# Projecting two kinds of keys with the weights stationary, so that they come out transposed

## What is computed

```
p = t @ w_in                       # t: the 256 tokens, and the same for the 256 context rows
qa, ka, va, qb, kb, vb, ob, g = split(p)          # six of width 512, ob, 16 gate columns
y_a = neighbourhood_attention(qa, ka, va, kax, vax, rpb)           # 8 heads of 64
h_b = mlstm_bidirectional(axial_rope(qb), axial_rope(kb) * k_scale, vb, li, lf,
                          qbx, kbx * k_scale, vbx, lix, lfx)       # 4 heads of 128
y = concat([y_a, mlstm_readout(h_b, ob, head_g)]) @ w_out
# axial_rope: of each pair (x[2d], x[2d+1]) of a head, with the angle of token and d
#   out[2d] = x1 * cos - x2 * sin;  out[2d+1] = x1 * sin + x2 * cos
```

## Time and profile before

| | |
|---|---|
| time, median of 3 executions | 1587.98 us (1587.47 to 1588.07) |
| time of the profiled execution | 1587.57 us |
| its span in the profile | 1585.7 us |
| granted TensorE clock, mean | 0.999 |
| busy: PE / DVE / ACT | 99% / 74% / 49% |
| instructions: PE / DVE / ACT | 7994 / 1917 / 1246 |

### The profile page before, as it was taken

One profiled execution on the slowest core, in us unless ns is written; L12 is line 12 of the kernel. 1 busy time (PEld: TensorE's weight loads), 2 busy tenths in 40 slices (PEclk: granted clock), 3 DMA queues, 4 the chain that ended last, 5 costly groups with the idle time before them and its releaser, 6 DMA issues.

```text
span 1585.7 us, 20742 instructions
## 1 busy us (share of the span) xinstructions
PE 1564.3 (99%) x7994; PEld 1296.7 (82%) x7994; DVE 1172.3 (74%) x1917; ACT 777.9 (49%) x1246; POOL 70.5 (4%) x112
## 2 busy tenths in 40 slices
PE   7999999999999999999999999999999999999998
PEld 5787778888888888887777888888888888888887
DVE  7889899759986665477766888868877667666654
ACT  5767666532222222254556555445555463455552
POOL 2000000100000000030010100000000100010000
PEclk9999999999999999999999999999999999999999
DMA  9987676336656655252122777857777685555550
GB/s 378 371 294 275 230 253 222 107 127 231 214 211 239 225 213 176 90 175 80 67 95 74 292 293 289 314 216 266 257 285 269 211 304 188 171 202 188 187 188 33
DMA packets 93044, 336.97 MB, mean 212 GB/s; under 512 B 10625, under 2 KB 11265, under 8 KB 92690
## 3 DMA queue, kind: packets, MB, share of 16 engines
q1 hardware_dynamic: 90706, 327.58, 57.5%
q0 software_dynamic: 2240, 8.06, 1.5%
HBM read 334.56 MB, written 1.05 MB: 212 GB/s over the span
## 4 chain that ended last, share of the span: by engine, by line
PE 55%; DVE 1%; ACT 1%; issue 0%; POOL 0%; POOLq 0%; DVEq 0%; ACTq 0%
PE bank L292 53%; PE bank L295 2%; DVE sb_tm L301 0%; ACT sb_XN L298 0%; DVE sb_X L301 0%; ACT sb_arena L298 0%; ACT sb_XC L298 0%; DVE sb_arena L319 0%; DVE sb_XN L301 0%; DVE sb_sg L316 0%; DVE sb_XC L301 0%; DVE sb_w7r L301 0%; DVE sb_w5r L301 0%; POOL sb_rstd L301 0%; DVE sb_rows L309 0%
## 5 line engine op out<-in xcount | busy, mean ns | idle before, releaser
L292 PE MATMUL bank<-sb_hT,sb_hi 128*128 128x512 f32 (+1 forms) x1856 | 574.9, 379 | 0.0
L298 ACT ACTIVATE sb_hi<-sb_w 128x1024 fp32r<-128x1024 f32 x428 | 431.3, 1052 | 281.8 <-DMA sb_w<-in_w 238.8
L292 PEld LDWEIGHTS bank<-sb_hT,sb_hi 128*128 128x128 f32 x1856 | 332.1, 188 | 58.5 <-issue 0.2
L292 PE MATMUL bank<-sb_hi,sb_hT 128*128 128x512 f32 x1152 | 369.6, 395 | 2.5 <-ACT sb_hT L298 1.3
L292 PEld LDWEIGHTS bank<-sb_hi,sb_hT 128*128 128x128 f32 x1152 | 215.6, 188 | 52.8 <-issue 5.3
L312 DVE CUSTOM_DVE_ANT_0 sb_w<-sb_w,sb_cb 128x1024 f32<-128x1024 f32 x144 | 174.7, 1218 | 0.0
L301 DVE TENSOR_TENSOR sb_sg<-bank,sb_sg 128x512 f32<-128x512 f32 (+1 forms) x90 | 58.9, 660 | 103.1 <-ACT sb_sg L298 82.2
L298 ACT ACTIVATE sb_sg<-bank 128x512 f32<-128x512 f32 (+1 forms) x98 | 55.0, 573 | 118.2 <-PE bank L292 117.7
L298 ACT ACTIVATE sb_arena<-bank 128x512 f32<-128x512 f32 (+1 forms) x106 | 56.4, 559 | 55.4 <-PE bank L292 32.3
L301 DVE TENSOR_TENSOR sb_tm<-bank,sb_rows 128x512 f32<-128x512 f32 (+1 forms) x41 | 28.1, 684 | 69.4 <-PE bank L292 66.5
L298 ACT ACTIVATE sb_XN<-sb_X 128x512 f32<-128x512 f32 x33 | 20.7, 629 | 99.2 <-DVE sb_X L301 91.3
(11 more groups left out here) (483 smaller groups left out, 3209.7 us busy)
## 6 DMA issues: line engine op xcount, KB each, us to landing
sb_w<-in_w SPq DMA_DIRECT2D x428, 512.0 KB, 4.3
sb_w<-in_mw SPq DMA_DIRECT2D x192, 512.0 KB, 4.7
sb_rows<-in_na_rpb POOLq DMA_DIRECT2D x16, 96.0 KB, 3.0
sb_X<-in_x SPq DMA_DIRECT2D x1, 1024.0 KB, 4.9
sb_cb<-in_cvec POOLq DMA_DIRECT2D x2, 512.0 KB, 8.8
sb_XC<-in_ctx POOLq DMA_DIRECT2D x1, 1024.0 KB, 13.0
sb_arena<-in_sg_ln_g POOLq DMA_DIRECT2D x1, 1024.0 KB, 7.1
sb_arena<-in_sg_ln_b POOLq DMA_DIRECT2D x1, 1024.0 KB, 10.4
```

The costliest lines, as they stand in the source:

```text
L292: return self.e.matmul(out, a, b, start=start, stop=stop)
L298: return self.e.activation(out, a, f, **kw)
```

## The change

Two kinds, mk and nk, are projected by a new function `pe_across`: the weights are stationary, the activations of the tokens and the context (both at once, 2 x 256 columns) are moving. Each of the four banks then holds 128 features on partitions and all 512 rows. The number of matmuls and their shape stay. No transposes, and no copies to `XN` and `XC`, are left for these kinds.

The memory keys' rotation then runs over partitions. The host permutes the columns of mq and mk in w_in, so that of each head the first members of the pairs lie in partitions 0 to 63 and the second ones in 64 to 127. `dve_keys` reads each pair of banks with three multiplications, one of 128 partitions by the cosine and two of 64 partitions that write the other half's partitions by the sine, and one sum. The table `axt` (128 x 512) comes by a new DMA on GpSimd's queue. ACT copies the context half of mk (`act_keys`). For nk, ACT copies each bank to `nkh` and DVE subtracts to `nkl`, after the last score of the mLSTM (`SCO ml 3 1`). Banks of mk are set free by the third multiplication of a pair, those of nk by the subtractions. The queries nq are split as soon as they are turned, behind tile 7. `sig`, the gate of the readout, moves to another place of the arena, so its evacuation waits for `PVS ml 3 1`.

```diff
-        MX = {5: [("cx", (0, 1))], 6: [("cx", (2, 3))], 7: [("t", ("nq", 0))], 8: [("gates", 0)],
-              9: [("gs", 0)], 10: [("t", ("mq", 0)), ("gs", 1)], 11: [("gs", 2)], 12: [("t", ("mk", 2)), ("t", ("mk", 0))],
-              13: [("pf", 0)]}
+
+
+        MX = {5: [("cx", (0, 1))], 6: [("cx", (2, 3))], 7: [("t", "nq")], 8: [("gates", 0)],
+              9: [("gs", 0)], 10: [("t", "mq"), ("gs", 1)], 11: [("gs", 2)], 13: [("pf", 0)]}
...
-        MX[20] += [("nqs", 0)]
-        MX[21] += [("t", ("nk", 0)), ("t", ("nk", 2)), ("nb", 0)]
+        MX[21] += [("nb", 0)]
...
+            if kind == "mk":
+                return (DE, "mk", "read", j // 2)
+            if kind == "nk":
+                return (DE, "nk", j)
+            return (AE, "mx", kind, j)
...
+                elif u < 28 and kind in ("mk", "nk"):
+                    pe_across(e, W_MX + u, key, at, BANK[key], ready)
                 elif u >= 4:
                     pe_unit(e, W_MX + u, key, parts, at, BANK[key], range(n), ready, first, last)
...
+        def pe_across(e, t, key, k0, banks, ready):
+
+
+            w, l = HI_[HB[t]], ring_r[SLOT["w", t]]
+            e.wait_ge(*done(HI, t))
+            for g in range(4):
+                c, b = slice(g * 128, g * 128 + 128), banks[g]
+                if k0 == 0:
+                    for f in b.free():
+                        e.wait_ge(*f)
+                for k in range(2):
+                    kc = k0 + k
+                    for f in ready(kc, "h", range(4)):
+                        e.wait_ge(*f)
+                    e.mm(b.ap[:, :], w[:, k, c], hTh[:, :, kc, :], kc == 0, False)
+                    for f in ready(kc, "l", range(4)):
+                        e.wait_ge(*f)
+                    e.mm(b.ap[:, :], w[:, k, c], hTl[:, :, kc, :], False, False)
+                    e.wait_ge(*done(LO, t))
+                    m = e.mm(b.ap[:, :], l[:, k, c], hTh[:, :, kc, :], False, kc == 7)
+                if g == 3:
+                    m.then_inc(USED.sem, USED.put(t))
+                    if k0 == 6:
+                        ENDED[(*key, g)] = (USED, t)
+                elif k0 == 6:
+                    m.then_inc(ACC.sem, ACC.put(*key, g))
+                    ENDED[(*key, g)] = (ACC, *key, g)
...
+        def act_keys(e, kind):
+            for g in range(4 if kind == "nk" else 2):
+                if kind == "nk":
+                    e.wait_ge(*ended("mx", "nk", g))
+                    e.act(nkh[:, g, :], BANK["mx", "nk"][g].ap[:, :], ACT.Copy).then_inc(AE.sem, AE.put("nk", g))
+                else:
+                    for j in (2 * g, 2 * g + 1):
+                        e.wait_ge(*ended("mx", "mk", j))
+                    e.act(mkT[:, 2 * g:2 * g + 2, 256:512], banks2[g][:, :, 256:512], ACT.Copy).then_inc(AE.sem, AE.put("mk", g))
+
+        def dve_keys(e, kind):
+            if kind == "nk":
+                e.wait_ge(*done(SCO, "ml", 3, 1))
+                for g in range(4):
+                    e.wait_ge(*done(AE, "nk", g))
+                    e.tt(nkl[:, g, :], BANK["mx", "nk"][g].ap[:, :], nkh[:, g, :].bitcast(F32), ALU.subtract).then_inc(
+                        DE.sem, DE.put("nk", g))
+                return
+            e.wait_ge(*done(LD["axt"], 0))
+            for g in range(2):
+                b, o = banks2[g][:, :, 0:256], mkT[:, 2 * g:2 * g + 2, 0:256]
+                w = TM[g].rearrange("p (a b) -> p a b", a=2)
+                co, si = (axt[:, i, :].unsqueeze(1).to_broadcast([128, 2, 256]) for i in range(2))
+                e.wait_ge(*done(AE, "mk", g))
+                e.wait_ge(DE, DE.n)
+                e.tt(o, b, co, ALU.mult).then_inc(DE.sem, DE.put("mk", "cos", g))
+                e.tt(w[0:64], b[64:128], si[64:128], ALU.mult).then_inc(DE.sem, DE.put("mk", "first", g))
+                e.tt(w[64:128], b[0:64], si[0:64], ALU.mult).then_inc(DE.sem, DE.put("mk", "read", g))
+                e.wait_ge(DE, DE.n)
+                e.tt(o, o, w, ALU.add).then_inc(DE.sem, DE.put("mk", g))
```

More of the change, by code:

```diff
@@ L2199, in build, with queries_ready, keys_ready, memory_ready @@
         MX[31] += [("gate", 0), ("y", 1)]
[L2201 to L2208, removed]
+        def queries_ready():
+            return [done(DE, "nq", 1)]
+        def keys_ready():
+            return [done(DE, "nk", 3)]
+        def memory_ready():
+            return [done(AE, "t", "mq", 0), done(DE, "t", "mq", 1), done(AE, "mk", 1), done(DE, "mk", 1)]
         def mx_tile(u):
@@ L2250, in pe_mixer @@
                     elif what == "t":
[L2251 to L2256, removed]
+                        w = [done(DE, "axial", "mq", 3)] if i == "mq" else [done(AE, "mx", "nq", j) for j in range(2)]
+                        pe_transposes(e, ("t", i), TQ[i == "mq"], 0, 4, w, TB,
+                                      lambda c2, i=i: ((DE, "nq", c2) if i == "nq" else (DE if c2 else AE, "t", "mq", c2),))
                     elif what == "pf":
@@ L2356, in pe_mlstm @@
                 if ph == 0:
-                    for f in all_turned("mq") + all_turned("mk"):
+                    for f in memory_ready():
                         e.wait_ge(*f)
@@ L2526, in pe_neighbour_scores @@
                 b = BANK["nS", i] = HB3.take()
-                for f in b.free() + [done(AE, "nqs"), done(DE, "nqs")] + all_turned("nk"):
+                for f in b.free() + queries_ready() + keys_ready():
                     e.wait_ge(*f)
@@ L2688, in act_mixer @@
                         act_gate_sums(e, i)
[L2689 to L2698, removed]
                     elif what == "t":
[L2700 to L2703, removed]
+                        for c2 in range(2 if i == "nq" else 1):
+                            e.wait_ge(*done(TRP, "t", i, c2))
+                            e.act((nqh if i == "nq" else mqT)[:, c2 * 2:c2 * 2 + 2, :], pair(BANK["t", i, c2]), ACT.Copy).then_inc(
+                                AE.sem, AE.put("t", i, c2))
                         act_tick(e, W_MX + u)
@@ L2803, in dve_mixer @@
                         dve_neighbour_bias(e, 1)
[L2804 to L2808, removed]
-                        for c2 in range(2):
[L2810 to L2815, removed]
+                    elif what == "t" and i == "nq":
+                        for c2 in range(2):
+                            c = slice(c2 * 2, c2 * 2 + 2)
+                            e.wait_ge(*done(AE, "t", "nq", c2))
+                            e.tt(nql[:, c, :], pair(BANK["t", "nq", c2]), nqh[:, c, :].bitcast(F32), ALU.subtract).then_inc(
+                                DE.sem, DE.put("nq", c2))
                     elif what == "t":
[L2817 to L2820, removed]
+                        e.wait_ge(*done(TRP, "t", "mq", 1))
+                        e.cp(mqT[:, 2:4, :], pair(BANK["t", "mq", 1])).then_inc(DE.sem, DE.put("t", "mq", 1))
                     elif what == "o":
@@ L3137 @@
     put("gb", a["ml_gate_b_2"].reshape(8, 2))
-    consts, blk, mlm = shape_constants()
+    consts, blk, mlm, axt = shape_constants()
+    mix = np.array(a["mix_w_in_2"])
+    for kind in ("mq", "mk"):
+        c = slice(BASE2[kind], BASE2[kind] + 512)
+        mix[..., c] = mix[..., c].reshape(-1, D, 4, 64, 2).transpose(0, 1, 2, 4, 3).reshape(-1, D, 512)
+    a = dict(a, mix_w_in_2=mix)
     w = np.stack([np.concatenate([a[name][ix][r:r + 256, n:n + 512 // len(ns)] for n in ns], axis=1)
```

63 lines of the change are left out of this document (31 added, 32 removed).

## The result

The changed kernel takes 1585.43 us (median of 21 runs, 1585.04 to 1585.97), the kernel before 1587.71 us (21 runs, 1587.45 to 1588.07): 2.28 us less, a ratio of 0.9985 with a 95% interval of 0.9979 to 0.9992. The forecast was 1585.5, 2.4 us less than before.

A forecast was written before the change was run, and what follows sets the result against it. PE, busy 99% of the span, was taken to bound the kernel. The terms -3.49 - 0.90 + 1.80 + 0.19 = -2.4 us gave 1585.5 us from a median of 1587.98; the 8-in-10 range was 1583.9 to 1587.2.

The forecast's parts named there:

- Transposes: PE, behind tiles 12 and 21: 32 transposes go, 16 at each, 1.75 and 1.74 us, in sum -3.49 us.
- Swapped operands: Tiles 8 to 11 and 16 to 19: 192 matmuls with weights stationary keep the 0.227 us pace, so 0.
- The rival of a slower pace: Swapped matmuls might not stream at 0.227 us; at 0.26 the kernel takes 1592 us; chance 0.05.
- Score block: Head 0's first score block: its waits for mkT's last copies and sb_fcol go, -0.90 us, bounds 0.5 and 0.9.
- Tile 12: New PE wait for banks freed by DVE's third multiplication, and again at the third bank: +1.80 us, between 1.36 and 2.16.
- The middle case: Tile 12: each DVE operation starts only when the one ahead has ended, 0.70 us apart, so three end at 722.27.
- Tile 20: PE waits for bank 0 until the first nkl subtraction, behind head 3's last score, ends: +0.19 us, bounds 0 and 0.3.
- What is late next: Head 3's chain on DVE, pushed 2.0 us later by four subtractions, still has slack before PE needs it: 0.
- the second place: Transposes at 796.74, waiting for the later result of head 3's chain: about 1.0 us of slack left.
- the first place: 16 matmuls at 789.49, said to wait for the first stretch of head 3's chain: 1.1 us of slack left.
- The rest of the kernel moves along: From 870 us on nothing is late, PE busy 709 of 715 us: the mixer's gain moves the rest forward whole.
- The time: Whole kernel: 1585.5 us, 2.4 less than before; chance 0.74 of the same within 0.2%, 0.22 faster, 0.04 slower.

The follow-up runs named there:

- e5: Changed kernel plus 16 more 128x128 transposes, of data that nothing reads, behind tile 21: 1587.15 us.
- e6: Changed kernel, but ACT also copies the memory keys' token half to SBUF, freeing the banks, and DVE rotates from the copy: 1584.53 us.
- e1: Changed kernel, but DVE rotates the memory keys of tile 11 before the weight split w2r, not behind it: 1584.51 us.
- e3: Changed kernel, but both 64-partition multiplications read and write partitions 0 to 63: 1584.93 us.
- e7: Changed kernel with three more DVE operations of 128x512 between the subtractions of nkl and head 3's chain: 1586.48 us.
- e2: Changed kernel with the edits of e1 and e6, and DVE's split of w0r moved behind the copy of sb_fcol: 1583.41 us.
- e4: Kernel before, with the change made for the memory keys alone, neighbourhood keys and queries as before: 1587.15 us.

## Why the prediction was right

- **Transposes, -3.49 us.** Right: 1.74 at tile 21 in the table, and 1.72 for 16 more in e5. At tile 12 the 1.75 stand inside the column's +0.12.
- **Swapped operands, 0.** Right: pace 0.227, and up to tile 11 no difference beyond what two executions differ by. The rival of a slower pace has nothing for it.
- **Score block, -0.90.** Right in the mechanism (in e6 PE comes 1.9 us earlier and waits for `sb_fcol` again, in e1 a part of that), 0.08 too large: the undisturbed block of head 0 takes 1.91 us for its four matmuls, while I took head 3's 1.81. The 2.18 us that I gave to six matmuls are those of four.
- **Tile 12, +1.80.** Right in mechanism and nearly in size: 1.87. The start is late by 1.57 us (1.44 forecast), the restart took 0.08 (0.11), the third bank 0.14 (0.25), and 0.08 came from a slightly slower pace that I had not in the sum. These errors, +0.13, -0.03, -0.11 and +0.08, mostly undo each other, so that the term is closer than its parts. Of the 0.13, 0.10 is that PE started 0.15 us behind DVE's end and not 0.05. The middle case for the operations' pace (0.70) was the right choice of the three; 0.72 was measured, and e3 brings it to 0.60 by changing nothing but the halves.
- **Tile 20, +0.19.** Right in mechanism, 0.03 to 0.05 too small. The subtraction ran as forecast; PE started 0.15 us behind its end, not 0.05. The score matmuls alone end near 783.3; the two selections that the prediction names with them only start there, and the subtraction doesn't wait for them.
- **What is late next.** The slack at the second place was right (1.0 us, e7), the first place wrong: I took the 16 matmuls at 789.49 to wait for the stretch of DVE that stands ahead of them in time, and e7 shows that they don't. This error had no effect on the forecast, since both places were given slack.
- **The rest of the kernel moves along.** Right: the shift at 870 us is that at 800 within 0.1 us in all kernels.

- **The time, 1585.5 us.** The gain was forecast 0.18 us too large by the trace: 0.08 in the score block, 0.07 at tile 12, 0.03 at tile 20. That 1585.5 came within 0.1 us is luck. It was built on 1587.98, the median of three runs, where 21 runs gave 1587.71, and -2.4 from 1587.98 is nearer 1585.6. Measured against the kernel before, the time fell by 0.15%, inside the 0.2% to which the prediction gave a chance of 0.74.

For mk, the transposes that went and the wait that came were thus about equal, and what the change brings is nk's transposes and the score block. e2 shows the loss to be no price of the idea: it came from the order in which DVE and ACT read the banks.

The Trainium skill ("VectorE: DVE Perf Modes", Two Vector instructions with no wait between them) says, as a model, that an instruction whose start quadrant isn't that of the previous read or write is held until every earlier one has finished; a quadrant is 32 partitions. The traces agree: 0.72 us from start to start where the halves change, 0.60 where they don't (e3), with the reservation made at e3. For transposes, the 275 ns that the Trainium skill gives in a kernel's context ("TensorE: Matmul & The Clock Gate", Part 4: PE-mode transpose; for bf16) are near the duration of 0.27 us that the rows show here for fp32, but not the cost, which e5 puts at 0.11.

## What to carry to other kernels

When an edit removes copies out of PSUM, look at who frees the banks afterwards and where that instruction stands in its engine's queue: here the matmuls that went were paid for with the wait for a bank whose reader stood behind a weight split. If another engine is idle at that time, let it free the banks and do the slow work from its copy, as ACT does in e6 and e2. When a wait is removed, compute the next one behind it at once (here `sb_fcol`, needed two tiles later, took back half): e1 and e6 gave 0.9 us each, and e2, which also removes the next wait, gave 2.0.

## What was unexpected

- PE starts 0.15 us behind the end of a DVE operation of 512 columns that frees a bank (722.18 to 722.32 at tile 12, 783.20 to 783.35 at tile 20), but 0.06 behind the copy of `sb_fcol` (733.75 to 733.81 in e6) and 0.05 in the earlier trace rows. No run here tells what makes the difference.
- Tile 12's matmuls start 0.231 us apart on average, in a pattern of 0.224 to 0.236, in the changed kernel, e1 and e4; in e2 and e6, where PE didn't wait for these banks, and for most of the tile in e3, where it did, it is 0.227. That is 0.1 us a tile. In e5 and e7, whose tile 12 is that of the changed kernel, the pace is back at 0.227 five matmuls behind each wait, so it isn't a fixed property of the code. Its cause stays open.
